# Block two of a two-block transformer layer: low weight parts summed by GpSimd DMAs, and the long convolution wholly on VectorE

## The reference, cut to what matters

```python
z = rmsnorm(h) @ w_in                      # 1024 x 7752, read in slices
c_a, c_g, q, k, v, qi, ki, wi, gc, ga = split(z)
u = c_a * sigmoid(c_g)                     # 256 x 1024
u = causal depthwise convolution of u, 31 taps, + conv_b
u = silu(layernorm(u)) @ w_conv_out
y_attn = attention over keys chosen by (qi, ki, wi) @ w_attn_out
h = h + (sigmoid(gc + b) * u + sigmoid(ga + b) * y_attn) @ w_mix_out
```

## Time and profile before

| | |
|---|---|
| median of 3 runs | 924.94 us (924.5 to 925.67) |
| span of the profiled execution, first to last instruction | 922.9 us |
| median less span | 2.0 us |
| TensorE's mean granted clock | 0.998 |
| PE busy | 915.0 us |
| DVE busy | 684.2 us |
| ACT busy | 523.9 us |
| POOL busy | 13.2 us |

### The profile page before, as it was taken

How to read it: one execution, slowest core, us unless ns; L and a number is a source line. 1 busy time by engine, 2 the same in 40 slices (tenths; PEclk the granted TensorE clock), 3 DMA queues, 4 the chain that set the end, 5 groups by cost and what they waited for, 6 DMA issues and landing times.

```text
span 922.9 us, 14161 instructions
## 1 busy us (share of the span) xinstructions
PE 915.0 (99%) x5373; PEld 788.7 (85%) x5373; DVE 684.2 (74%) x1188; ACT 523.9 (57%) x899; POOL 13.2 (1%) x17
## 2 busy tenths in 40 slices
PE   9999999999999999999999999999999999999997
PEld 7899987788888888888899988888788888888886
DVE  6879976368766666678688989998786776666666
ACT  7656767755654444555545436754946674545444
POOL 0300000000000000000000000000000000000000
PEclk9999999999999999999999999999999999999999
DMA  9954545565465555554654945555475346655551
GB/s 342 323 151 143 158 135 166 186 222 187 152 214 200 194 191 195 191 184 153 203 174 143 250 130 155 176 174 177 140 234 187 99 161 223 215 183 183 183 183 45
DMA packets 91026, 168.54 MB, mean 183 GB/s; under 512 B 7568, under 2 KB 14032, under 8 KB 90704
## 3 DMA queue, kind: packets, MB, share of 16 engines
q1 hardware_dynamic: 90592, 167.13, 56.0%
q10 hardware_dynamic: 368, 0.52, 0.2%
HBM read 164.77 MB, written 1.05 MB: 180 GB/s over the span
## 4 chain that ended last, share of the span: by engine, by line
PE 95%; DMA 2%; DVE 1%; ACT 0%; SPq 0%; issue 0%; DVEq 0%; ACTq 0%
PE pb L451 93%; PE pb L455 3%; DMA raw<-in_w_in 2%; DMA raw<-in_w_first 1%; DVE wlo L1621 0%; ACT QKV L1053 0%; SPq L384 0%; SPq L387 0%; DVE XT L2156 0%; DVE ST L1797 0%; DVE wlo L2167 0%; ACT SQ L1215 0%; ACT whi L1053 0%; DVE X L2361 0%; DVE MSQ L2399 0%
## 5 line engine op out<-in xcount | busy, mean ns | idle before, releaser
L1621 DVE TENSOR_TENSOR wlo<-raw,whi 128x1024 fp32r<-128x1024 f32 (+1 forms) x298 | 353.8, 1213 | 113.4 <-ACT whi L1053 112.9
L1053 ACT ACTIVATE whi<-raw 128x1024 fp32r<-128x1024 f32 (+1 forms) x304 | 309.1, 1039 | 153.1 <-PE pb L451 128.1
L451 PE MATMUL pb<-XT,whi 128*128 128x256 f32 (+2 forms) x1456 | 312.9, 330 | 0.8 <-ACT QKV L1053 0.6
L451 PEld LDWEIGHTS pb<-XT,whi 128*128 128x128 f32 (+1 forms) x1456 | 239.7, 190 | 21.6 <-issue 2.6
L451 PE MATMUL pb<-whi,ZO 128*128 128x512 f32 (+1 forms) x808 | 251.8, 389 | 0.0
L451 PE MATMUL pb<-XT,wlo 128*128 128x256 f32 (+1 forms) x1032 | 209.2, 282 | 0.0
L451 PEld LDWEIGHTS pb<-whi,ZO 128*128 128x128 f32 x808 | 151.3, 188 | 31.6 <-DVE wlo L1621 1.1
L451 PEld LDWEIGHTS pb<-XT,wlo 128*128 128x128 f32 (+1 forms) x1032 | 167.9, 190 | 8.7
L451 PE MATMUL pb<-whi,XT 128*128 128x512 f32 (+1 forms) x544 | 170.7, 390 | 0.5 <-ACT whi L1053 0.4
L451 PE MATMUL pb<-wlo,ZO 128*128 128x512 f32 (+1 forms) x404 | 156.6, 388 | 0.0
L451 PEld LDWEIGHTS pb<-whi,XT 128*128 128x128 f32 x544 | 101.3, 188 | 21.7 <-issue 0.9
(11 more groups left out here) (247 smaller groups left out, 592.0 us busy)
## 6 DMA issues: line engine op xcount, KB each, us to landing
raw<-in_w_in SPq DMA_DIRECT2D x105, 512.0 KB, 3.7
raw<-in_w_ff SPq DMA_DIRECT2D x64, 512.0 KB, 5.1
raw<-in_w_up SPq DMA_DIRECT2D x32, 512.0 KB, 4.6
raw<-in_w_down SPq DMA_DIRECT2D x32, 512.0 KB, 5.3
raw<-in_w_branch_b SPq DMA_DIRECT2D x8, 512.0 KB, 5.9
raw<-in_w_out SPq DMA_DIRECT2D x8, 512.0 KB, 3.7
raw<-in_wx_kv SPq DMA_DIRECT2D x8, 512.0 KB, 5.3
raw<-in_w_attn_out SPq DMA_DIRECT2D x8, 512.0 KB, 4.2
```

The source lines that it names most:

```text
L451: return e.matmul(o, l, r, start=start, stop=stop, skip_group_check=True)
L1053: return e.activation(o, i, ACT.Copy, scale=scale)
L1621: e.tensor_tensor(wlo[u % NW][:, 0:c], raw[u % NRAW][:, 0:c], whi[u % NW][:, 0:c].bitcast(F32), ALU.subtract).then_inc(lo, 1)
```

## The change

- Of the 49 units `b2_qi` to `b2_ga0` all but `b2_ki` (so 48) get their low part in another way. ACT, right after `whi`, writes `-whi` into `wlo` (a second activation of the same size). POOL waits for that and issues a DMA that adds `raw` onto it (`accum_op=ADD`, 512 KB, SBUF to SBUF). TensorE and SP wait for that DMA's semaphore in the place of `lo`. DVE's `make_lo` does nothing for these units.
- TensorE's convolution, with `WQ`, `U4`, its 16 DMAs, `conv_blocks`, `conv_outs`, its tap table in the parameters and all their waits, is gone. DVE makes all eight tiles, two at a time, 248 operations in the place of 155, dealt out over the 50 places by a list, `TAPS2`.

```diff
+TAPS2 = (7, 8, 7, 7, 5, 7, 7, 7, 4, 7, 4, 7, 0, 7, 4, 4, 3, 4, 4, 4, 4, 4, 3, 6, 7, 7, 7, 7, 8, 7, 4, 7, 3, 7, 4, 7, 2, 7, 3, 7, 0, 7, 2, 7, 0, 7, 6, 1, 0, 0)
...
+        hi_negated, lo_summed = sem("w_hi_negated"), [sem(f"w_lo_summed{i}") for i in range(NW)]
+        by_dma = [u for u in range(first["b2_qi"], first["b2_ga1"]) if u != first["b2_ki"]]
+        lo_at, n_lo, n_sum = [], 0, [0] * NW
+        for u in range(len(units)):
+            if u in by_dma:
+                n_sum[u % NW] += 16
+                lo_at.append((lo_summed[u % NW], n_sum[u % NW]))
+            else:
+                n_lo += 1
+                lo_at.append((lo, n_lo))
...
-                if u == b2 + 28:
-                    e.wait_ge(*out_at["b2_ca1", 3])
-                    e.wait_ge(u4_zero, 1)
-                if b2 + 28 <= u < b2 + 32:
-                    j = u - b2 - 28
-                    a = 1 if j == 0 else 0
-                    for g in range(4):
-                        e.dma_start(U4[32 * j:32 * j + 32, :, g, a:284],
-                                    U2[32 * g:32 * g + 32, PE_CONV:8, j + a - 1:j + 283]).then_inc(u4_in, 16)
...
-                e.wait_ge(lo, u - NRAW + 1)
+                e.wait_ge(*lo_at[u - NRAW])
                 load(u)
...
             def weights(u):
-                e.wait_ge(lo, u + 1)
+                e.wait_ge(*lo_at[u])
                 return weight_tiles(u)
...
-            def conv_taps():
...
-                for n in range(8 - PE_CONV):
-                    e.wait_ge(wq_made, n + 1)
-                    if n >= 2:
-                        e.wait_ge(cv_out, n - 1)
-                    for q in range(8):
-                        for g in range(4):
-                            i = mm(PB[6 + n % 2][32 * g:32 * g + 32, 0:256], WQ[n][:, q, g, :],
-                                   U4[:, n, g, 4 * q:4 * q + 256], q == 0, q == 7)
-                    i.then_inc(cv_done, 1)
...
                 copy(whi[u % NW][:, 0:c], raw[u % NRAW][:, 0:c]).then_inc(hi, 1)
+                if u in by_dma:
+                    e.wait_ge(hi, u + 1)
+                    copy(wlo[u % NW][:, 0:c], whi[u % NW][:, 0:c].bitcast(F32), -1.0).then_inc(hi_negated, 1)
...
-            def conv_outs():
...
-                    if name == "b2_q0":
-                        e.wait_ge(cv_done, 2)
...
                 made[0] += 1
+                if u in by_dma:
+                    return
...
-            def conv_blocks():
...
-                places = itertools.chain(*([q] * n for q, n in enumerate((3,) * 8 + (2,) * 15 + (6,) * 7 + (3,) * 20)))
+                places = itertools.chain(*([q] * n for q, n in enumerate(TAPS2)))
                 made, at = {}, 0
-                for fs in ((0, 1), (2, 3, 4)):
+                for fs in ((0, 1), (2, 3), (4, 5), (6, 7)):
...
-                                if at == 28:
-                                    sum_tiles((0, 1, 5, 6, 7), y_made, 2)
+                                if at == 24:
+                                    sum_tiles((0, 1), y_made, 2)
+                                if at == 36:
+                                    sum_tiles((2, 3), y_made, 4)
...
             def conv_norm():
-                sum_tiles((2, 3), y_made, PE_CONV)
+                sum_tiles((4, 5, 6), y_made, 8)
                 after_step()
-                e.tensor_tensor(LNS[0], LNS[0], YC[:, 4, :], ALU.add).then_inc(ln_tiles, 1)
+                e.tensor_tensor(LNS[0], LNS[0], YC[:, 7, :], ALU.add).then_inc(ln_tiles, 1)
...
-            e.wait_ge(cv_done, 8 - PE_CONV)
...
             norm(N_MIX)
+            for i, u in enumerate(by_dma):
+                c = units[u][1] * units[u][2]
+                e.wait_ge(hi_negated, i + 1)
+                e.dma_start(wlo[u % NW][:, 0:c].bitcast(F32), raw[u % NRAW][:, 0:c],
+                            accum_op=ALU.add).then_inc(lo_summed[u % NW], 16)
             norm_both(N_XA)
```

More of the change, by code:

```diff
@@ L26 @@
                   ("lng", 8), ("lnb", 8), ("normx", 8), ("normmem", 8), ("normffn", 8), ("qg", 1), ("kg", 3),
-                  ("posk", 16), ("posv", 16), ("convq", 128)):
+                  ("posk", 16), ("posv", 16)):
     PRM[_name] = _n
@@ L30 @@
 NPRM = _n
-CS = {"ident": 0, "ones": 128, "dist": 256, "causal": 640, "mhalf": 1024, "eye4": 1025, "end": 1057}
+CS = {"ident": 0, "ones": 128, "dist": 256, "causal": 640, "mhalf": 1024, "end": 1025}
 C2 = {"cbias": 0, "cmask": 512, "end": 1024}
@@ L45 @@
 GAIN = {T_X: "norm1", T_MEM: "normmem", T_2: "norm2", T_MIX: "normmix", T_XA: "normx", T_FFN: "normffn"}
-PE_CONV = 5
+TAPS2 = (7, 8, 7, 7, 5, 7, 7, 7, 4, 7, 4, 7, 0, 7, 4, 4, 3, 4, 4, 4, 4, 4, 3, 6, 7, 7, 7, 7, 8, 7, 4, 7, 3, 7, 4, 7, 2, 7, 3, 7, 0, 7, 2, 7, 0, 7, 6, 1, 0, 0)
 HALVES = ("b1_c0", "mk", "b2_cg0", "b2_ca0")
@@ L122, in build @@
         YC = work(W0 + 8432, "YC", 2048)[:, :].rearrange("p (f n) -> p f n", f=8)
-        U4 = ZO[:, 0:4 * 284 * (8 - PE_CONV)].bitcast(F32).rearrange("p (f g n) -> p f g n", g=4, n=284)
-        WQ = [work(W0 + a, f"WQ{i}", 1024)[:, :].rearrange("p (q g c) -> p q g c", q=8, g=4)
-              for i, a in enumerate((0, 1024, 16240))]
         QI = work(W0 + 12784, "QI", 1024)[:, :].rearrange("p (f n) -> p f n", f=4)
@@ L340, in build @@
         wi_t, wi_out, ki_moved = sem("wi_turned"), sem("wi_copied"), sem("ki_moved")
-        wq_made, u4_zero, cv_done, y_made, cv_out = (sem(x) for x in (
-            "conv_blocks_made", "u4_zeroed", "conv_tile_done", "y_made", "conv_copied"))
-        u4_in = sem("u4_landed")
+        y_made = sem("y_made")
         ln_tiles, ln_sum, ln_mu, ln_sub, ln_sq, ln_sqs, ln_var, ln_sd, ln_norm, silu_done = (sem(x) for x in (
@@ L829, in ffn @@
                         down(tag, c - 1, lambda j: (t_lo, t_at[s, j]))
-            def conv_taps():
-                for _ in range(15):
-                    yield
-                e.wait_ge(u4_in, 256)
-                for n in range(8 - PE_CONV):
-                    e.wait_ge(wq_made, n + 1)
-                    if n >= 2:
-                        e.wait_ge(cv_out, n - 1)
-                    for q in range(8):
-                        for g in range(4):
-                            i = mm(PB[6 + n % 2][32 * g:32 * g + 32, 0:256], WQ[n][:, q, g, :],
-                                   U4[:, n, g, 4 * q:4 * q + 256], q == 0, q == 7)
-                    i.then_inc(cv_done, 1)
-                    yield
-                    yield
             def attention2():
@@ L885, in attention2 @@
                         e.wait_ge(*out_at[f"b2_v{h // 4}", 1])
-                        e.wait_ge(*(o_lo, 4 + h) if h else (cv_out, 8 - PE_CONV))
+                        if h:
+                            e.wait_ge(o_lo, 4 + h)
                         o = PB[6]
@@ L942, in tensor_program @@
             i.then_inc(unit_done, 1)
-            side, taps = attention2(), conv_taps()
+            side = attention2()
             for name in ("b2_cg1", "b2_ca1", "b2_k0", "b2_k1", "b2_q0", "b2_q1"):
-                cols(name, XT, ready, side, taps)
+                cols(name, XT, ready, side)
             for name in ("b2_v0", "b2_v1", "b2_gc0", "b2_gc1"):
-                rows(name, XT, ready, side, taps)
+                rows(name, XT, ready, side)
             norm = conv_norm()
-            rows("b2_ga0", XT, ready, side, taps)
-            now(taps)
+            rows("b2_ga0", XT, ready, side)
             rows("b2_ga1", XT, ready, side, norm)
@@ L1497, in scalar_program @@
             e.dma_start(KI[64:128, :], KW[0:64, :]).then_inc(ki_moved, 16)
-            side, outs = attention2(), conv_outs()
+            side = attention2()
             for name in ("b2_cg1", "b2_ca1", "b2_k0", "b2_k1", "b2_q0", "b2_q1"):
-                run(name, side, outs)
+                run(name, side)
                 if name == "b2_cg1":
@@ L2044, in scale_keys @@
                     yield
-            def conv_blocks():
[L2047 to L2052, removed]
             def sum_tiles(fs, done, n):
                 e.wait_ge(done, n)
-                e.wait_ge(cv_out, 8 - PE_CONV)
                 o = LNS[0]
@@ L2246, in vector_program @@
                 make_t_lo(T_MIX, j, XT)
-            run("mv", conv_blocks(), scale_keys())
+            run("mv", scale_keys())
             step(e.memset(U2[:, :, 0:30], 0.0))
@@ L2255, in vector_program @@
             conv_in0()
-            e.memset(U4[0:32, :, :, 0:1], 0.0).then_inc(u4_zero, 1)
             taps = taps2()
@@ L2471, in constants @@
     c[:, CS["mhalf"]] = -0.5
-    c[np.arange(P), CS["eye4"] + np.arange(P) % 32] = 1.0
     q, k = np.arange(P)[:, None], np.arange(2 * P)[None, :]
@@ L2506 @@
         params[:, PRM[name]:PRM[name] + v.shape[1]] = v
-    w = np.zeros((32, D), np.float32)
-    w[1:] = I["conv_w_2"].reshape(31, D)
-    params[:, PRM["convq"]:] = w.reshape(8, 4, 8, 4, 32)[:, :, 4:].transpose(1, 4, 2, 0, 3).reshape(P, 128)
     for r in (0, 64):
```

## The result

The changed kernel takes 951.4 us in the median of 4 runs (947.8 to 955.7), against 925.0 before: a ratio of 1.0285, 95% interval 1.0265 to 1.0305. The forecast was 942 us with a range of 913 to 965; the direction is right and the loss is 26 us where 17 were forecast. The profiled execution is the fastest of the four, with a span of 945.8 us.

A forecast was written before the change was run, and what follows sets the result against it. TensorE bounded the kernel before; full DMA engines would bound it after. Twelve groups at 15.0 us plus 2.8 make the stage 182.8 us for 165.5, +17.3: span 940.2, time 942 us, range 913 to 965.

The forecast's parts named there:

- TensorE's 10.9 us: Stage of the change: TensorE's three convolution blocks go, -10.9 us, all on the bounding chain.
- The price of an addition: Accumulating DMAs: two reads at a load's price, 2.68 us of all engines; bounds 1.34 and 6.6 us.
- The overlap: DMA engines: packets of two queues overlap by 1.07, so 4.02 us of packet time gives 3.75 us a unit.
- The sum: Stage of the change: 12 x 15.0 + 2.8 = 182.8 us in the place of 165.5, +17.3 us.
- 4 x 3.75 = 15.0 us: Each group of four units lasts the longer of its TensorE time and this DMA time.
- DVE and ACT: DVE: -55 us of low parts, +37 us of taps, off the path; ACT: 1.08 us more a unit, counted as nothing.
- Rival B: Accumulations cheap, under 2.27 us of packet time each; TensorE stays the bound: 913 to 921 us, chance 0.38.
- Rival C: After copied groups, a landing over 6.5 us stalls TensorE; at 8.0, 10.5 us in all: 918 to 932, chance 0.11.
- Rival D: Far dearer additions, by POOL's issue or `U4` copy prices: near 1002 or about 1115 us, chance 0.08.
- The signs: Profile after: DMA share near 1, some 280 GB/s, DMA onto `wlo` in the chain, units 3.75 us apart, landings 7 us or more.

The follow-up runs named there:

- copy run: Changed kernel with the 48 GpSimd DMAs copying `raw` onto `wlo` instead of adding it, all waits, sizes and queues kept: 915.6 us.
- the small negation: Changed kernel with ScalarE negating only 8 of the 1024 columns of each unit, DMAs untouched: 949.1 us.
- the taps alone: Changed kernel with all eight tiles on VectorE, but all low parts made by VectorE as before, no `-whi` and no adding DMAs: 949.6 us.
- the run with 12 sums: Kernel before with two tiles left on TensorE, six on VectorE, and 12 of the 48 low parts summed by DMA: 922.2 us, ratio 0.9964.
- the versions with a share of 0.95 and more: Fewer additions: thirty sums with no tile on TensorE, 926.2 us; 27 sums with one tile on TensorE, 923.6 us.
- those at 0.76 to 0.88: Fewer additions: 21 or 19 sums with one tile on TensorE, 922.2 and 922.3 us; 12 sums with two tiles, 922.2 us.

## Why the prediction was right, point by point

- **TensorE's 10.9 us.** Shown by the copy run: 915.6 us with everything but the addition in place, and 10.4 us less for TensorE to do. The first term was right, and in the changed kernel TensorE was no longer the bound, as forecast.
- **The price of an addition.** Forecast 2.68 us of all engines, measured 2.70; the plain copy 1.37, about half. The choice between 1.34 and 6.6 was made by row length and two operands. The first half is shown: a copy with 4 KB rows costs what a load does, and not the 3.3 of `U4`'s rows. That the cost is twice a copy's is shown too. That it is the second read which costs, as the Trainium skill has it ("Collectives: The Full Stack", The bandwidth ceiling: the fold count and why AG ≠ RS ≠ AR), fits the copy run but wasn't separated from the addition itself.
- **The overlap.** Forecast 1.07, measured 1.06.
- **The sum.** The span grew by 22.9 us, not 17.3. (165.5 + 22.9 - 2.8) / 48 is 3.87 us a unit. So the step that was too small is "4 x 3.75 = 15.0 us" a group: it measured 15.5. The term behind it is the load's. 1.34 us is its wall time at a share of 1.03, so 1.38 of packet time, which is what the sum adds up. And in 462 to 640 us of the changed kernel the loads' queue, with two of the four gate bias loads that I had left out, took 38.1% for 24.56 MB, 1.45 us for each 0.524 MB. (1.45 + 2.70) / 1.06 = 3.91 us a unit; the 48 additions were issued 3.9 us apart in the mean (184.5 us for 47 steps). The overlap and the price were each slightly kind besides (2 us and 1 us).
- **The other 3.6 us** of the median lie above the profiled execution. The spans of the four runs are 945.8, 948.7, 949.9 and 953.9 at mean granted clocks of 0.999, 0.991, 0.993 and 0.990. The three longer ones have the lower clocks, but only the first run has rows, so that the clock makes them longer is not shown. I had no term for it.
- **DVE and ACT.** Right, both have room. ACT's second activation shows no cost: the small negation took 35 us of work from it and the time stayed. That DVE's relief covers the 93 taps is shown from the other side by the taps alone (949.6).
- **Rival B** needed an addition under 2.27 us. The copy run, at 1.37, is that rival come true: 915.6 for the 915 given. The Trainium skill's fit for a GpSimd DMA ("DMA: Bandwidth & Descriptors", Anatomy of one DMA — SWDGE (gpsimd) path) would make the landing 3.2 us; under this load the copies landed after 5.1 us in the median and 3.0 at best, the additions after 8.2 and 4.7.
- **Rival C** was never tested by itself: with landings of 5.1 and 5.5 us, under its 6.5, TensorE hardly waited. In the run with 12 sums the landings take 6.7 at a share of 0.76 and TensorE doesn't wait, but none of the 12 is the conversion right behind a group's copies, where C would bite. **Rival D** is out: GpSimd's issue is 0.87 us, and no addition of the changed kernel took over 10.5 us to land. (Its high bound of 7.4 us a unit adds up to about 1118, not 1115.)
- **The signs.** Right: a DMA share of 1.05 to 1.06 in every 20 us of the stage, 270 GB/s for some 280, landings of 8.2 us, the DMAs onto `wlo` in the chain.
- **Wrong in detail:** I expected TensorE to idle before nearly every unit and bare units 3.75 us apart. The rows have 26 waits in 460 to 640 us, in which 45 additions were issued; the five buffers come round in bursts.

## What to carry to other kernels

When work moves from an engine to DMA, put the bytes of the DMA engines on the same balance sheet as the engines' busy time, by the window in which they fall: here an accumulating SBUF-to-SBUF DMA of 512 KB cost 2.70 us of all 16 engines, twice a copy, where a load costs 1.38 to 1.45 with the engines full and TensorE's own pace was 3.2 a unit. Then dose it. Here the versions with a share of 0.95 and more came out even or worse than before, though the sum gave them a gain; those at 0.76 to 0.88 won 0.3 to 0.4%, and only the one at 0.76 came out about as computed. Read the share with care, though: in 560 to 580 us of before it is 0.55 at 169 GB/s, which is 1.7 us of packet time for a load, while the same load costs 1.38 to 1.45 where the engines are full. By these rows, half-empty engines have more room than their share says. And count the small transfers that share the queue, since the late gate bias held an in-order engine, and that engine held TensorE.

## What the runs showed of the hardware that I had not expected

- With four transfers' buffers in the place of five, full engines moved 250 GB/s and not 270, and an addition took 2.81 us for 2.70.
- Halving an addition's bytes by halving its rows from 4 KB to 2 KB left 57% of its cost (1.54 for 2.70 us).
- GpSimd stood 0.87 us at an accumulating DMA and 0.54 us at a plain one of the same shape.
- TensorE's granted clock read 0.50 in the 2 us windows from 506 to 514 us of the taps-alone run, in and behind an idle stretch of 10.1 us. In the profiled execution of the changed kernel it stayed at 1.00 in all windows of 20 us, with PE busy for only 13.46 us in one of them and no single wait over 2.8 us. Executions of the changed kernel spread over 8 us, those of the kernel before over 1.2; a link between the two isn't shown.
- A load's packets took 1.38 us of all engines for 512 KB in the loads-only stretch of the earlier trace rows, 1.45 beside the additions, and 1.7 in 560 to 580 us of before, where the engines were half idle.
